# One-hot passes of the gated side moved from VectorE to ScalarE, chunks two beats apart

## What is computed

```python
def peer_block(xb, wq, keys, u_tab, v_tab):            # xb: 128 tokens
    q = (xb @ wq).reshape(T, 8, 2, 128)
    s = jnp.einsum('thpc,hpkc->thpk', q, keys)
    sv, si = lax.top_k(s, 16)                          # per head, two lists of 16 keys
    best, pos = lax.top_k(all 256 pair sums, 16)       # 16 experts a head
    idx  = key_a * 128 + key_b                         # (128 tokens, 128 experts)
    gate = softmax(best)
    act  = gelu(einsum('ted,td->te', u_tab[idx], xb)) * gate
    return einsum('te,ted->td', act, v_tab[idx])
```

## Time and profile before

| | |
|---|---|
| median of 3 runs | 3376.09 us (3374.08 to 3394.76) |
| profiled execution | 3380.35 us, span of the trace 3378.5 us |
| TensorE busy | 2914.1 us (86%) |
| VectorE busy | 1746.1 us (52%) |
| ScalarE busy | 515.7 us (15%) |
| GpSimd busy | 1544.5 us (46%) |
| moved by DMA | 999 MB, mean 296 GB/s |

### The profile page before, as it was taken

The page is one execution under the profiler, slowest core; times in us unless marked ns, Lnnn a source line. Parts: engine busy times, 40 slices in busy tenths (PEclk is TensorE's granted clock), DMA queues, the critical chain, the costliest instruction groups (busy, mean ns, idle before and its releaser), DMA issues.

```text
span 3378.5 us, 29554 instructions
## 1 busy us (share of the span) xinstructions
PE 2914.1 (86%) x10143; PEld 1469.8 (44%) x10143; DVE 1746.1 (52%) x3906; ACT 515.7 (15%) x1064; POOL 1544.5 (46%) x1335
## 2 busy tenths in 40 slices
PE   6999987676699879745679999999999999999996
PEld 4656556332234335423424444444444444444431
DVE  4431138787986465599746644555634434341111
ACT  3111032200100045445600000000000000000000
POOL 2202121554576545455654555545555555543343
PEclk9999988787899979867889999999999999999998
DMA  3322442896799988878999999999899999998776
GB/s 115 94 87 89 138 163 77 307 325 229 240 381 371 385 342 304 313 274 295 403 402 349 356 351 350 371 381 362 319 365 370 375 347 370 363 363 306 281 285 225
DMA packets 336621, 999.03 MB, mean 296 GB/s; under 512 B 31735, under 2 KB 107383, under 8 KB 334168
## 3 DMA queue, kind: packets, MB, share of 16 engines
q0 software_dynamic: 184320, 671.17, 53.0%
q1 hardware_dynamic: 150424, 300.80, 25.1%
q10 hardware_dynamic: 1728, 25.17, 1.8%
HBM read 948.52 MB, written 48.50 MB: 295 GB/s over the span
## 4 chain that ended last, share of the span: by engine, by line
PE 55%; DVE 9%; DMA 9%; issue 4%; ACT 3%; POOL 2%; another core or an unknown queue 0%; SPq 0%; DVEq 0%; ACTq 0%; POOLq 0%
PE job_ps L1388 19%; PE wide_ps L1372 18%; PE v_ps L1409 7%; DMA v_rows<-in_peer_v,row_t 3%; PE wide_ps L548 3%; PE job_ps L548 3%; DVE prod L1628 2%; PE wide_ps L1360 2%; POOL u_row L1297 2%; DMA u_row<-in_peer_u,row_u 1%; DMA tmp_gates<-arena 1%; ACT arena L1487 1%; DVE prod L187 1%; DVE prod L182 1%; DMA arena<-tmp_gates 1%
## 5 line engine op out<-in xcount | busy, mean ns | idle before, releaser
L1307 POOL DMA_INDIRECT v_rows<-in_peer_v,row_t x640 | 682.8, 1067 | 816.8 <-PE v_ps L1409 633.4
L1297 POOL DMA_INDIRECT u_row<-in_peer_u,row_u x640 | 739.7, 1156 | 511.8 <-DVE dots L1628 290.6
L1628 DVE CUSTOM_DVE_ANT_0 prod<-u_row,x_tile 128x1024 f32<-128x1024 f32 x640 | 765.7, 1220 | 106.0 <-DMA u_row<-in_peer_u,row_u 94.7
L1388 PE MATMUL job_ps<-arena 128*128 128x512 f32 x1536 | 690.5, 598 | 6.1 <-DVE arena L1666 5.3
L1372 PE MATMUL wide_ps<-xd_t,arena 128*128 128x384 f32 x2048 | 688.3, 490 | 6.9 <-DMA arena<-in_peer_ut 6.9
L1372 PEld LDWEIGHTS wide_ps<-xd_t,arena 128*128 128x128 f32 x2048 | 385.5, 190 | 326.7 <-issue 79.1
L1388 PEld LDWEIGHTS job_ps<-arena 128*128 128x128 f32 x1536 | 288.6, 191 | 377.2 <-issue 340.7
L1409 PE MATMUL v_ps<-v_rows,diag 128*32 128x512 f32 x2560 | 363.7, 613 | 57.2 <-DMA v_rows<-in_peer_v,row_t 56.6
L1666 DVE TENSOR_TENSOR arena<-arena,job_ps 128x512 f32<-128x512 f32 x192 | 131.8, 687 | 488.8 <-PE job_ps L1388 440.9
L791 POOL TENSOR_TENSOR exact<-arena,exact 128x1024 fp32r<-128x1024 f32 x48 | 117.1, 2442 | 431.5 <-ACT exact L560 431.5
L1514 ACT ACTIVATE arena<-wide_ps 128x384 f32<-128x384 f32 x128 | 62.9, 491 | 1450.0 <-PE wide_ps L1372 1149.5
(11 more groups left out here) (239 smaller groups left out, 2252.6 us busy)
## 6 DMA issues: line engine op xcount, KB each, us to landing
arena<-in_peer_ut SPq DMA_DIRECT2D x128, 512.0 KB
arena<-in_peer_v SPq DMA_DIRECT2D x128, 512.0 KB
arena<-in_w_in SPq DMA_DIRECT2D x64, 512.0 KB, 3.5
tmp_gates<-arena ACTq DMA_DIRECT2D x12, 2048.0 KB
arena<-tmp_gates SPq DMA_DIRECT2D x32, 768.0 KB
arena<-in_w_o SPq DMA_DIRECT2D x32, 512.0 KB, 3.5
arena<-in_wq SPq DMA_DIRECT2D x32, 512.0 KB, 3.6
u_row<-in_peer_u,row_u POOLq DMA_INDIRECT x640
```

Source lines behind the costliest of these rows:

```text
L1297: pool.indirect_dma_start(u_row[n % NU][:], None, dram["peer_u"], bass.IndirectOffsetOnAxis(row_u[g % 2][:, e:e + 1], 0)).then_inc(u_in[n ...
L1307: pool.indirect_dma_start(v_row[n % NV], None, dram["peer_v"], bass.IndirectOffsetOnAxis(row_t[g % 3][:, t:t + 1], 0)).then_inc(v_in[n % N ...
L1388: last = pe.matmul(job_ps[q % 2][:], actd[g % 2][:, jj, d * P:(d + 1) * P], vw[j % NO][:, half * 512:(half + 1) * 512], start=jj == 0, sto ...
L1628: dve.tensor_tensor_reduce(out=prod[n % 2][:], in0=u_row[n % NU][:], in1=xb[g % 2][:], scale=1.0, scalar=0.0, op0=ALU.mult, op1=ALU.add, a ...
```

## The change

All 48 chunks have their `hot_b` made by ScalarE. The eight VectorE passes of sixteen chunks (17, 19, ... 47) and their semaphore `d_done` go; `BY_ACT` and `BY_DVE` go with them. VectorE keeps the batched compare. From chunk 16 on chunks start two beats apart, where they were one and two in turn: chunk 31 moves from beat 284 to 292, chunk 32 from 289 to 295, chunk 47 from 311 to 325. The dense stage's start follows `CHUNK_AT[-1]`, from beat 317 to 331, its end does not move, and `PACE` falls from 5.79 to 5.58 ticks.

```diff
-    CHUNK_AT += [CHUNK_AT[-1] + 7 + c + c // 2 for c in range(EARLY)]
-    CHUNK_AT += [max(CHUNK_AT[-1], GATED_AT[5]) + 3 + c + c // 2 for c in range(EARLY)]
-    BY_ACT = [c for c in range(CHUNKS) if c < EARLY or c % 2 == 0]
-    BY_DVE = [c for c in range(CHUNKS) if c not in BY_ACT]
+    CHUNK_AT += [CHUNK_AT[-1] + 7 + 2 * c for c in range(EARLY)]
+    CHUNK_AT += [max(CHUNK_AT[-1], GATED_AT[5]) + 3 + 2 * c for c in range(EARLY)]
...
                 pe.wait_ge(a_done, c + 1)
-                if c in BY_ACT:
-                    pe.wait_ge(b_done, BY_ACT.index(c) + 1)
-                else:
-                    pe.wait_ge(d_done, BY_DVE.index(c) + 1)
+                pe.wait_ge(b_done, c + 1)
...
-                act.wait_ge(sq_done, BY_ACT.index(c) + 1)
+                act.wait_ge(sq_done, c + 1)
...
-                        if n == CHUNK_AT[c] and c in BY_ACT:
+                        if n == CHUNK_AT[c]:
                             hot_square(c)
                             hot_relu(c)
...
-                if c in BY_DVE:
-                    for v in range(8):
-                        last = dve.tensor_scalar(hot_b[c % 2][:, v], R.iota[:], sel_t[d % 2][:, 1, t0 + v:t0 + v + 1],
-                                                 gate_t[d % 2][:, t0 + v:t0 + v + 1], ALU.is_equal, ALU.mult)
-                    last.then_inc(d_done, 1)
```

More of the change, by code:

```diff
@@ L1188, in second_and_experts @@
             "exp_done", "gel_done", "act_done", "act_turned", "diag_done", "v_used", "lead_done", "gate_done"))
-        sel_turned, sel_copied, a_done, sq_done, b_done, d_done, hot_used, evicted = (m.sem(f"e_{n}") for n in (
-            "sel_turned", "sel_copied", "a_done", "sq_done", "b_done", "d_done", "hot_used", "evicted"))
+        sel_turned, sel_copied, a_done, sq_done, b_done, hot_used, evicted = (m.sem(f"e_{n}") for n in (
+            "sel_turned", "sel_copied", "a_done", "sq_done", "b_done", "hot_used", "evicted"))
         u_used, gel_read, weighted, job_done, summed = (m.sem(f"e_{n}") for n in (
```

## The result

| | before | after |
|---|---|---|
| median | 3378.86 us (6 runs, 3374.08 to 3394.76) | 3409.88 us (6 runs, 3401.03 to 3415.12) |
| profiled execution | 3380.35 us | 3414.28 us |
| ratio of after to before | | 1.0083, 95% interval 1.0057 to 1.0108 |

A forecast was written before the change was run, and what follows sets the result against it. VectorE was taken to bound 1485 to 1565 us, TensorE from 1790 on. Terms -15.7 + 0 + 44.1 + 5 - 8 - 6.7 = +18.7 us gave 3399.1 against the profiled 3380.35; forecast 3395 us, range 3375 to 3425.

The forecast's parts named there:

- Term 1: Beats 262 to 280: VectorE, which sets the pace, loses six one-hot groups and three compares; -15.7 us.
- Term 2: Ranking at beat 280: VectorE's work, unchanged, ending with ScalarE's Exp; 0 us.
- Terms 3 and 4: Beat 280 to last eviction: ScalarE becomes the bound, 22 chunks at 6.57 us, +44.1 us; late rows from transfers, +5 us.
- Term 5: Hand-over to the dense stage, sooner with full rings, -8 us; quads of 14 more beats already done, -6.7 us.
- There TensorE is full and order, not pace, decides: Dense stage: squeezing its pace from 5.79 to 5.58 ticks was given no cost.
- Rival A: After the ranking: TensorE's products come late, a chunk takes 7.6 us; +45 us, 3421 us; chance 0.25.
- Rival B: Dense stage bound by transfers: 14 beats already done return 41 us; -16 us in all, 3360 us; chance 0.08.
- Rival C: No change overall: VectorE relief and a full -17 us hand-over largely pay ScalarE's longer chain; +5 us, 3381; chance 0.12.

The follow-up runs named there:

- close_early_evict: act_close with the evictions of the last sixteen chunks two beats behind their passes instead of three; 3390.51 us, ratio 1.0057 to the kernel before.
- beats_only: The kernel before with only the changed chunk beats, odd chunks' second one-hots still made by VectorE; 3409.52 us, ratio 1.0095.
- short_square: The changed kernel with seven of eight Square passes left out in odd chunks from 33 on; 3408.59 us, ratio 1.0088 to the kernel before.
- acc_later: The changed kernel with SP's 1.5 MB load of `acc` moved behind the first dense loads; 3410.31 us, ratio 1.0069 to the kernel before.
- old_line: The changed kernel, chunks untouched, with dense products from 8 on back at the beats of the kernel before; 3399.15 us, ratio 1.0041.
- act_close: The changed kernel with its last sixteen chunks one beat apart instead of two; 3449.66 us, ratio 1.0196 to the kernel before.
- shared_chunks: late_split with the last sixteen chunks one beat apart, one-hots split four and four, evictions two beats behind, dense line adjusted; 3351.36 us, ratio 0.9946.
- late_split: The kernel before, its beats kept, with ScalarE making all second one-hots of chunks 0 to 31; 3374.43 us, ratio 0.9976.

## Why the prediction came out right, and what in it was wrong

The measured +0.83% lies in the range and in the case with the largest chance (within 1%), near its upper edge. Between the medians it is +31 us, just inside the forecast's band of +10 to +33; between the profiles it is +33.9, just outside. That the time stayed in the band was partly luck: two steps failed, both on the side of too fast. By its own terms, against the profiles:

- **Term 1** (-15.7): measured -14.9. Right: VectorE's removed passes and compares came back almost whole, since it was the bound there, and it stayed the bound. The sign given for it, that VectorE would no longer be over 95% busy from 1485 us on, did not show: it is busy 76.5 of 80 us in after. An engine that bounds a stretch stays full when work is taken from it; the stretch becomes shorter.
- **Term 2** (0): right; the ranking ends with the Exp, for which ScalarE waits 12.0 us, 10.9 before.
- **Terms 3 and 4** (+44.1 and +5): measured +45.5 together. The price of a chunk was right, 6.57 us forecast, 6.52 measured; the wait of ScalarE for products went, as the order said. Of what they were said to show, one half is incomplete: "ScalarE becomes the bound" is true, and close_early_evict shows that it suffices for the loss in this stage, but it is not the only cause. With ScalarE's load halved and the same beats the stage is as long (153.3 us, beats_only). Two bounds lie on each other at 6.5 us a chunk. Term 4 saw this ("the transfers are just at the level ScalarE asks for") but gave it a price for being late instead of seeing a second bound of the same height. Someone who followed term 3 alone would have taken work from ScalarE and gained 4 us of 16 in the stage, and nothing that the total shows (short_square).
- **Term 5**, hand-over (-8): this step failed, and measured 0; product 8, too, stands no sooner behind the last eviction, 113.9 us in after for 112.7 before. I had VectorE at beat 331 some 6 us before the last eviction, with both rings full. Its last dot product ahead of the first weighing ended at 1729.8 us, 13.6 after that eviction: a third routed head, at beat 330, also falls here, which I had left out, and rows came late. In after GpSimd still issued fetches until 1735.6 us. The rings were not full, and the weight loads had as much beside them as before.
- **Term 5**, quads (-6.7): -5.5 from product 0 to 104, right. Counted off, 72 quads stand there in after where before has 75, and 3 x 1.92 = 5.8 us. The stage scatters more than that from kernel to kernel: beats_only and short_square, with the same beats, have -10.3 and -10.6, acc_later -3.8.
- **"There TensorE is full and order, not pace, decides"**: this sentence priced the squeeze of the dense line at nothing, and it cost 12.7 us from product 104 to the last quad; old_line gives 10 of them back. TensorE is full until about 2957 us, but in the last 420 us it idles 44 even before the change, and there it matters where the quads stand. I had read the stage from 1790 to 2600 and taken it for all that followed.

The two failures, 8 + 12.7 us, less what terms 3 and 4 were too high (3.6), make most of the 19 us by which the stages' sum (+37.9) exceeds the forecast (+18.7).

Rival A (TensorE late, 7.6 us a chunk) did not occur in after: ScalarE waited 3.1 us for products in the whole stage. It is what happened in act_close, once the order let it. Rival B (the dense stage gives the time back) is refuted: the 14 beats already done gave back 5.5 us, not 41. Rival C did not occur.

The Trainium skill's figure of about 358 GB/s from HBM for a core ("DMA: Bandwidth & Descriptors", Specifications) is not this stage's limit: beats_only moved 398 GB/s over 110 us, shared_chunks 401 over 80, both at a DMA share of 1.0. The same page of the Trainium skill says under Bandwidth, Measured, that 358 is each core's part when both cores of an HBM domain stream, and gives 425 GB/s for a core alone with transfers of 16 MB. Here one core runs, so the prediction had taken the wrong one of the two figures for its comparison. By 358 a chunk of after would have taken 7.3 us, an estimate; it took 6.9 on average (Squares from 1562.67 to 1707.28 us, 21 steps of 6.89).

The Trainium skill's rule that Relu, multiplies and adds belong on VectorE ("ScalarE: Activation LUTs", Rules for kernel authors) agrees with these rows on the price: a chunk's passes take 2.05 us on VectorE, in one instruction each, and 5.57 on ScalarE, in two. It does not decide where the work should stand: late_split moves VectorE work to ScalarE and is 0.24% faster. In the beats ahead of the ranking VectorE was busy 77 of 80 us and ScalarE 44.

## What to carry to other kernels

When a resource is found full, look for a second one at the same height before calling it the cause: halve the load of the first, and if nothing moves, a second bound stands behind it, and what else is at a share of 1.0 is the first to suspect. Work that is spread between the steps of a starved stage costs what it takes in that stage, so put such a stage's steps as close as the engines allow and leave the filler to a stage that has room; but recheck the order in each queue, since a step that stands a fixed number of beats behind can come to stand behind the next one's work. When a schedule is squeezed, read its far end too.

## What the runs showed of the hardware that I had not expected

In act_close, with TensorE busy 37 of 90 us, the granted clock was 0.62 (nearer the 1.2 GHz level), and a chunk's 16 matmuls took 3.75 us instead of the 2.02 that they take where the granted clock is 1.00. So a serial order cost more than its durations at full clock say. And a stage near 400 GB/s moved about the same whatever traffic shared it: fetches of gathered rows and gate writes held 398 GB/s (beats_only), and with weight loads beside them, before, it was 400:

```profile
1690.00:1790.00 100.00, 74.67 (x237) 32.41 (x230) 51.80 (x153) 4.61 (x8) 54.51 (x50) 0.85 1.04 400
```
